# Column blocks in the neighbourhood attention, and VectorE for the rest of each weight unit

## The reference

```python
def _na_mixer(h, hc, w_in, rpb, w_out, need_ctx_out):    # h 512 tokens, hc 256
    q, k, v, g = jnp.split(h @ w_in, 4, axis=-1)          # 16 heads of 64; q * 64**-0.5
    kc, vc = jnp.split(hc @ w_in[:, WIDTH:3 * WIDTH], 2, axis=-1)
    row_idx = ...   # all 8 rows: the window is as high as the grid
    col_idx = clip(col - 8, 0, 64 - 16)[:, None] + arange(16)   # 16 of the 64 columns
    s_loc = (q . k in the window) + rpb[head, row distance, column distance]
    logits = concatenate([s_loc, q . kc], -1)             # 8*16 local keys, 256 context keys
    p = softmax(logits)
    return ((p_loc @ v + p_ctx @ vc) * silu(g)) @ w_out
```

## Time and profile before

| | |
|---|---|
| median of 3 runs | 3138.78 us (3133.11 to 3140.57) |
| the profiled execution, its own time | 3141.7 us |
| its span | 3139.9 us, 37990 instructions |
| mean granted TensorE clock | 0.964 of full speed |
| DMA | 287.38 MB, mean 92 GB/s |

### The profile page before, as it was taken

How to read it: one execution, slowest core, us unless ns; L and a number is a source line. 1 busy time by engine, 2 the same in 40 slices (tenths; PEclk the granted TensorE clock), 3 DMA queues, 4 the chain that set the end, 5 groups by cost and what they waited for, 6 DMA issues and landing times. The chain is left out here.

```text
span 3139.9 us, 37990 instructions
## 1 busy us (share of the span) xinstructions
PE 2919.9 (93%) x14938; PEld 2410.3 (77%) x14938; DVE 1757.9 (56%) x2601; ACT 970.3 (31%) x1552; POOL 803.6 (26%) x304
## 2 busy tenths in 40 slices
PE   7999999999998898888989999999999889999999
PEld 6776777777777776667868888888888668878887
DVE  4984766666645998976556566552233536431111
ACT  2223344444332222223234423122222334332222
POOL 0221212111134443431200022232222120134444
PEclk8998999999999999899989999999999899999999
DMA  5244332232124553432310033331111120022223
GB/s 209 84 148 122 99 93 92 73 99 73 65 101 168 167 168 113 142 114 73 104 58 1 1 101 108 119 104 64 63 61 61 46 81 1 21 74 94 96 98 101
DMA packets 110896, 287.38 MB, mean 92 GB/s; under 512 B 38720, under 2 KB 41888, under 8 KB 110208
## 3 DMA queue, kind: packets, MB, share of 16 engines
q1 hardware_dynamic: 108560, 281.03, 27.0%
q10 hardware_dynamic: 2160, 3.93, 0.4%
HBM read 278.90 MB, written 6.03 MB: 91 GB/s over the span
## 5 line engine op out<-in xcount | busy, mean ns | idle before, releaser
L705 POOL TENSOR_TENSOR w_lo<-w_raw,w_hi 128x1024 fp32r<-128x1024 f32 x300 | 803.4, 2679 | 2325.2 <-ACT w_hi L987 2325.1
L753 PE MATMUL turns<-h_hi,w_hi 128*128 128x512 f32 (+1 forms) x2480 | 811.0, 376 | 86.5 <-POOL w_lo L705 67.9
L753 PE MATMUL turns<-h_hi,w_lo 128*128 128x512 f32 (+1 forms) x2480 | 786.4, 366 | 0.0
L753 PE MATMUL turns<-h_lo,w_hi 128*128 128x512 f32 (+1 forms) x2480 | 784.0, 366 | 0.0
L753 PEld LDWEIGHTS turns<-h_hi,w_hi 128*128 128x128 f32 x2480 | 428.3, 194 | 202.7 <-POOL w_lo L705 89.4
L1204 DVE CUSTOM_DVE_ANT_0 ada_acc<-ada_raw,cond_rows,ada_bias 128x1024 f32<-128x1024 f32 x264 | 501.2, 1923 | 19.3 <-DMA ada_raw<-in_adapack 11.6
L753 PEld LDWEIGHTS turns<-h_hi,w_lo 128*128 128x128 f32 x2480 | 424.0, 193 | 76.3
L753 PEld LDWEIGHTS turns<-h_lo,w_hi 128*128 128x128 f32 x2480 | 425.4, 193 | 73.2 <-issue 1.4
L987 ACT ACTIVATE w_hi<-w_raw 128x1024 fp32r<-128x1024 f32 x300 | 315.4, 1051 | 407.0 <-PE turns L753 389.0
L1195 DVE SCALAR_TENSOR_TENSOR x_lat<-turns,modulation,x_lat 128x512 f32<-128x512 f32 x112 | 83.9, 749 | 413.7 <-PE turns L753 413.7
L753 PE MATMUL turns<-m_hi,w_lo 128*128 128x512 f32 (+1 forms) x768 | 233.4, 358 | 0.0
(11 more groups left out here) (199 smaller groups left out, 3585.1 us busy)
## 6 DMA issues: line engine op xcount, KB each, us to landing
w_raw<-in_wpack SPq DMA_DIRECT2D x300, 512.0 KB, 3.5
ada_raw<-in_adapack SPq DMA_DIRECT2D x176, 512.0 KB, 4.4
bias<-bias_table SPq DMA_DIRECT2D x32, 224.0 KB, 3.8
ada_first_a<-in_adapack SPq DMA_DIRECT2D x12, 512.0 KB, 8.7
bias_table<-bias_out ACTq DMA_DIRECT2D x16, 240.0 KB, 2.4
x_lat<-in_xT SPq DMA_DIRECT2D x1, 2048.0 KB, 8.6
x_ctx<-in_ctxT SPq DMA_DIRECT2D x2, 1024.0 KB, 8.8
ada_first_b<-in_adapack SPq DMA_DIRECT2D x4, 512.0 KB, 14.7
```

Source lines behind the costliest of these rows:

```text
L705: pool.tensor_tensor(Wl[:, b, :], RAW[:, b, :], Wh[:, b, :].bitcast(F32), ALU.subtract).then_inc(w_split, 1)
L753: ins = pe.matmul(dst[:, lo:lo + sz], w, x[:, lo:lo + sz], start=first and n == 0, stop=last and n == 2)
```

## The change

Two things are changed, and a third follows from the space that they need.

**The attention's blocks.** 128 queries are now 8 grid rows of 16 columns, one of four column blocks. Keys and values of the latent tokens are stored in the same order, so that a chunk of 128 keys is a column block too. Block 0 needs chunks 0 and 1, block 1 chunks 0 to 2, block 2 chunks 1 to 3, block 3 chunks 2 and 3, and each the two context chunks 4 and 5:

```diff
+NA_CHUNKS = ((4, 5, 0, 1), (4, 5, 0, 1, 2), (4, 5, 2, 3, 1), (4, 5, 2, 3))
+NA_PLACE = ((0, 1, 4, 5), (0, 1, 2, 4, 5), (4, 5, 1, 2, 3), (4, 5, 2, 3))
+NA_BIAS_AT, NA_BIAS_W = (0, 896, 256, 1280), 1792
# scores, TensorE: 256 or 384 latent columns and 256 of the context
+                            pe.matmul(SP_[:, 0, at_l:at_l + nl], x[:, q], y[:, k0:k0 + nl], start=n == 0, stop=n == 2)
+                            ins = pe.matmul(SP_[:, 0, at_c:at_c + TC], x[:, q], y[:, TX:TT], start=n == 0, stop=n == 2)
# softmax, VectorE and ScalarE: local and context scores lie side by side (nk = 512 or 640)
-                            dve.tensor_tensor_reduce(ex[:, 0:TX], SP_[:, 0, 0:TX], bias, 1.0, -3.0e38, ALU.add, ALU.max,
-                                                     st[:, 0:1])
-                            chain(dve.tensor_reduce(st[:, 1:2], SP_[:, 0, TX:TT], AX.X, ALU.max))
-                            give(dve.tensor_scalar(st[:, 2:3], st[:, 0:1], st[:, 1:2], -1.0, ALU.max, ALU.mult))
+                            give(dve.tensor_tensor_reduce(ex[:, 0:nk], SP_[:, 0, s0:s0 + nk], bias, -1.0, 3.0e38, ALU.add, ALU.min,
+                                                          st[:, 2:3]))
-                            act.activation(ex[:, 0:TX], ex[:, 0:TX], ACT.Exp, bias=st[:, 2:3], scale=1.0, accum_out=st[:, 3:4])
-                            give(act.activation(ex[:, TX:TT], SP_[:, 0, TX:TT], ACT.Exp, bias=st[:, 2:3], scale=1.0,
-                                                accum_out=st[:, 4:5]))
+                            give(act.activation(ex[:, 0:nk], ex[:, 0:nk], ACT.Exp, bias=st[:, 2:3], scale=-1.0,
+                                                accum_out=st[:, 3:4]))
-                            chain(tt(st[:, 5:6], st[:, 3:4], st[:, 4:5], ALU.add))
-                            chain(dve.reciprocal(st[:, 6:7], st[:, 5:6]))
+                        chain(dve.reciprocal(st[:, 6:7], st[:, 3:4]))
# values, TensorE: two blocks at once; a chunk that only one of them needs takes 128 columns
+                        wide = NA_CHUNKS[s.qt + 1 if s.qt == 0 else s.qt]
+                        for n, k in enumerate(wide):
+                            q = slice(0, 256) if n < 4 else slice(P, 256) if s.qt == 0 else slice(0, P)
+                            for j, (v, p) in enumerate(((Vh, PTh[0]), (Vh, PTl[0]), (Vl, PTh[0]))):
+                                ins = pe.matmul(PS[:, b, TT + q.start:TT + q.stop], v[:, k, :], p[:, n, q], ...)
```

The transposes become 4 or 5. Queries, keys, values and gate are put into the new order where they are evicted, and the result goes back into row order:

```diff
+        def by_cols(ap):
+            return ap.rearrange("p (b r c) -> p r b c", b=4, r=ROWS, c=WIN)
+        def by_rows(ap):
+            return ap.rearrange("p (r b c) -> p r b c", b=4, r=ROWS, c=WIN)
# ScalarE, q and k units (the v unit is likewise in two copies, 256 plain and 512 re-ordered)
-                        give(act.activation(dst, ps[:, 0:t], ACT.Copy, scale=0.125 if s.ev == "q" else 1.0))
+                        if s.ev == "k":
+                            act.activation(dst[:, TX:TT], ps[:, TX:TT], ACT.Copy)
+                            give(act.activation(by_cols(dst[:, 0:TX]), by_rows(ps[:, 0:TX]), ACT.Copy))
+                        else:
+                            chain(act.activation(by_cols(T1[:, 0:TX]), by_rows(ps[:, 0:TX]), ACT.Copy, scale=0.125))
+                            give(act.activation(dst[:, 0:TX], T1[:, 0:TX], ACT.Copy))
# ScalarE, g units
-                        give(act.activation(G2[:, s.pair % 2, :], ps[:, 0:t], ACT.Tanh, scale=0.5))
+                        act.activation(by_cols(T1[:, 0:TX]), by_rows(ps[:, 0:TX]), ACT.Copy)
+                        give(act.activation(by_cols(G2[:, s.pair % 2, :]), by_rows(ps[:, 0:t]), ACT.Tanh, scale=0.5))
# VectorE, k and q units
-                        done(rest(lo[:, p, 0:t], ps[:, 0:t], hi[:, p, 0:t], 0.125 if s.ev == "q" else None))
+                        if s.ev == "k":
+                            rest(lo[:, p, TX:TT], ps[:, TX:TT], hi[:, p, TX:TT])
+                            done(rest(by_cols(lo[:, p, 0:TX]), by_rows(ps[:, 0:TX]), by_cols(hi[:, p, 0:TX])))
+                        else:
+                            done(rest(lo[:, p, 0:TX], T1[:, 0:TX], hi[:, p, 0:TX]))
# the result of two blocks
-                        give(act.activation(Oh[r, s.tile, s.q0:s.q0 + 256], PVT[r, :], ACT.Copy))
+                        give(act.activation(blocks(Oh[r, s.tile, :], s.q0), paired(PVT[r, :]), ACT.Copy))
```

The bias of a head is laid out by the host as 128 x 1792 float32 (917 KB, zero for the context columns) and loaded once a head; the `bias_row` steps, their inputs, `bias_table` and the waits on them go:

```diff
-                        for r in range(2):
-                            sp.dma_start(BIAS[n % 2][r * 64:r * 64 + 64, :].rearrange("c (s j) -> c s j", j=GRID_W),
-                                         bias_d[n * NDR + 1 - r:n * NDR + 15 - r].rearrange("s c j -> c s j")
-                                         ).then_inc(bias_in[n % 2], 16)
+                        sp.dma_start(BIAS[n % 2][:], A["bias"][n]).then_inc(bias_in[n % 2], 16)
```

```diff
-        @block.gpsimd
-        def _(pool):
-            for w in range(n_units):
-                b = w % 2
-                pool.wait_ge(w_rounded, w + 1)
-                pool.tensor_tensor(Wl[:, b, :], RAW[:, b, :], Wh[:, b, :].bitcast(F32), ALU.subtract).then_inc(w_split, 1)
+            def split_unit(w):
+                if w < n_units:
+                    dve.wait_ge(w_rounded, w + 1)
+                    if w >= 2:
+                        dve.wait_ge(turn_mm, turn_of_w[w - 2] + 1)
+                    tt(Wl[:, w % 2, :], RAW[:, w % 2, :], Wh[:, w % 2, :].bitcast(F32), ALU.subtract).then_inc(w_split, 1)
...
+                if s.kind == "unit" and turn_of_w[s.w] == s.turn:
+                    split_unit(s.w + 2)
                 if s.ada and s.d1:
                     dve.wait_ge(dve_done, s.d1)
                 for sect, k in s.ada:
```

**Space.** `ada_acc` shrinks from two rows of 1024 to one. The last reduction of a chunk writes its full-width output over its own input (`ada_raw`), and `cond_rows` treats its two rows one after the other:

```diff
+                    dump = ACC[:] if c < both else ADR[:, n % 2, :]
+                    ins = dve.tensor_tensor_reduce(dump, ADR[:, n % 2, :], CROW[:, c, :], 0.5, ADAB[:, sect, k:k + 1],
                                                    ALU.mult, ALU.add, MOD[:, sect, c, k:k + 1])
-                dve.wait_ge(crow_tanh, n)
                 for c in range(2):
-                    ins = stt(CROW[:, c, :], ACC[:, c, :], 1.0, CROW[:, c, :], ALU.add, ALU.mult)
-                ins.then_inc(crow_made, 1)
-                dve.wait_ge(crow_made, n)
+                    dve.wait_ge(crow_tanh, 2 * n - 1 + c)
+                    stt(CROW[:, c, :], ACC[:], 1.0, CROW[:, c, :], ALU.add, ALU.mult).then_inc(crow_made, 1)
+                dve.wait_ge(crow_made, 2 * n)
```

More of the change, by code:

```diff
@@ L205, in na_scores @@
     def na_scores(n, q, k):
-        sc[n] = add("scores", na=True, pair=n // 8, half=n % 8 // 4, qt=n % 4, st=0, eb=n % 2, first=n % 4 == 0, nk=NT)
+        sc[n] = add("scores", na=True, pair=n // 8, half=n % 8 // 4, qt=n % 4, st=0, eb=n % 2, first=n % 4 == 0, nk=len(NA_CHUNKS[n % 4]))
         sc[n].after = [q, k]
     def na_trans(n):
-        tr[n] = add("trans", na=True, eb=n % 2, col=n % 2 * P, nk=NT, qt=n % 4)
+        tr[n] = add("trans", na=True, eb=n % 2, col=n % 2 * P, nk=len(NA_CHUNKS[n % 4]), qt=n % 4)
         tr[n].after = [soft[n - 1]]
@@ L468, in plan @@
     for s in steps:
-        n = {"hnorm": 0, "back": 0, "rope": 1, "vtrans": 1, "scores": s.st, "bias_row": s.st, "trans": 1 if s.na else None}.get(s.kind)
+        n = {"hnorm": 0, "back": 0, "rope": 1, "vtrans": 1, "scores": s.st, "trans": 1 if s.na else None}.get(s.kind)
         if n is not None:
@@ L607, in build_blocks @@
         na_pv_end = [s for s in by_kind["pv"] if s.na][-1]
-        last_gate0 = [s for s in by_kind["unit"] if s.ev == "gate"][KT - 1]
-        first_xupd = [s for s in by_kind["unit"] if s.ev == "xupd"][0]
         first_ctx2 = [s for s in by_kind["sq0"] if s.x0 == TX][0]
@@ L1425, in _ @@
                         take()
-                        done(rest(Ol[r, s.tile, q], PVT[r, :], Oh[r, s.tile, q]))
+                        done(rest(blocks(Ol[r, s.tile, :], s.q0), paired(PVT[r, :]), blocks(Oh[r, s.tile, :], s.q0)))
                     else:
@@ L1453, in _ @@
                         take()
-                        done(stt(G2[:, s.pair % 2, :], G2[:, s.pair % 2, :], 1.0, ps[:, 0:t], ALU.add, ALU.mult))
+                        done(stt(G2[:, s.pair % 2, :], G2[:, s.pair % 2, :], 1.0, T1[:, 0:t], ALU.add, ALU.mult))
                     elif s.ev == "cgate":
@@ L1562, in constants, with bias_places @@
     return c
+def bias_places():
+    at = np.full((ROWS, WIN, NA_BIAS_W), NDR * NDC + 1)
+    for b in range(4):
+        local = sorted(c for c in NA_CHUNKS[b] if c < 4)
+        at0 = NA_BIAS_AT[b] + (0 if b < 2 else TC)
+        for n, chunk in enumerate(local):
+            for r in range(ROWS):
+                for c in range(WIN):
+                    q = b * WIN + c
+                    first = min(max(q - WIN // 2, 0), GRID_W - WIN)
+                    for rk in range(ROWS):
+                        for jc in range(WIN):
+                            j = chunk * WIN + jc
+                            ok = first <= j < first + WIN
```

(2 more changed lines are left out.)

125 lines of the change are left out of this document (48 added, 77 removed).

## The result

The changed kernel takes 3026.3 us (median of 4 runs, 3024.0 to 3035.7), the kernel before 3139.7; ratio 0.9646, 95% interval 0.962 to 0.967. I had forecast 3057 with a range of 3022 to 3098. So the sign and the order are right, and the gain is 113 us where I had worked out 82. The result lies only 4 us inside the lower end of the range and outside the 3040 to 3077 that I gave the likeliest case.

What follows compares the result with a forecast made beforehand. TensorE, busy 93%, was taken to bound most stages, with slack in four stretches and GpSimd's subtraction stalling VectorE. The terms sum to -82 us from 3141.7, giving 3059.9, or 3057 against the median; range 3022 to 3098.

Steps and rivals of the forecast that it cites:

- head, conditioning rows: Conditioning rows, now made one after the other with one scratch: +0.8 us.
- first pool layer, u and gate units: Pool mixer's u units: VectorE now waits for ScalarE's eviction and rounding before subtracting, against the removed stall: +8.7 us.
- bias rows: First pool layer: without its 16 computed bias rows the output projection starts earlier: -16 us (-10 to -18).
- attention: Smaller score, value and transpose work, shorter softmax: -5.6 us in each of seven pairs, last pair -10; -49 (-25 to -75).
- projections and gates that VectorE paces: Output projections of convolution, second pool layer and attention, and second pool gates, lose GpSimd's stall: -15 us (-8 to -25).
- convolution: VectorE loses GpSimd's stalls, TensorE then binds, 182 us against 199: -17 us (-8 to -22).
- second pool layer, u units: VectorE's new wait costs +0.66 us each, 5.3, less 2.1 because first gate units get w_lo sooner: +3.2 us.
- sk and sq, first layer of the second block: Attention and MLP input: rounding, subtraction and reductions end after each other, TensorE waits: +6.5 us (0 to +12).
- all other pairs, norms, second block: First pairs of a stage, where w_lo comes 1 to 1.5 us sooner, with second-block norms: -4 us (0 to -8).
- rival 2: Clock comes back: shorter waits no longer bring it down in the attention and partly the convolution; 3032 us, chance 0.15.
- Rival 1: Attention's gain stays idle: softmax chain sets all steps, -26 there, strided writes up to twice plain rate; about 3085, chance 0.20.
- Rival 3: Subtraction slow on VectorE, 2.44 us instead of 1.22, wherever VectorE paces: +122, 3180 us, chance 0.04.

Runs made afterwards that it cites:

- g: Changed kernel with modulation chunks before the subtraction in units ScalarE evicts alone, and between x update and sum of squares in output projections: 2970.6 us.
- b: Kernel before, with only the w_lo subtraction moved from GpSimd to VectorE; attention, bias table and scratch as before: 3097.5 us, ratio 0.986.
- j: Changed kernel plus five multiplications of constants (256 columns each, never read) on TensorE before the scores of each attention step: 3132.2 us, ratio 0.998.
- k: Changed kernel plus one or two unread multiplications of constants, in turn, on TensorE before the scores of each attention step: 3049.0 us, ratio 0.972.

## Why the forecast came out as it did

Each term of the sum, with what the two profiles show between the same roundings (negative is faster):

| step of the prediction | forecast | measured |
|---|---|---|
| head, conditioning rows | +0.8 | -5.7, by the clock's rise |
| first pool layer, u and gate units | +8.7 | +6.9 |
| bias rows | -16 | -18.6 |
| attention | -49 | -57.9 |
| projections and gates that VectorE paces | -15 | -17.8 |
| convolution | -17 | -18.3 |
| second pool layer, u units | +3.2 | +8.3, their first pair included |
| sk and sq, first layer of the second block | +6.5 | +11.4 |
| all other pairs, norms, second block | -4 | -26.0 |
| sum | -82 | -117.7 |

The head's -5.7 is luck. g has the changed kernel's head, its clock rises at 30.9 us as in the profile of before, and its third rounding starts at 95.03 against 94.35: +0.7, close to the forecast +0.8.

*Right.* The price of the subtraction (1.22 us forecast, 1.22 measured); the reductions at 1.28 (1.24 forecast); MLP units at 8.47 and 5.47; the stages in which the change loses, because VectorE now waits for ScalarE's rounding, and that they are the u, sk and sq units; the bias rows; the convolution. That the gain at the output projections is ordinary pacing is seen in their period: 6.78 became 6.03.

*Losses forecast too small.* Here the clock went the other way. At sk and sq TensorE's idle time grew by 6.7 us, close to the 6.5 of the sum, but the lower level also grew, from 6.8 to 20.5 us, and busy time with it by 4.7: the stage is 11.4 longer. In the second pool layer's u units the idle time grew by 5.2 us (5.3 forecast before I took 2.1 off for the gates) and the lower level by 6.8.

*Attention, 9 us more gain than forecast.* The chain came out about as worked out, the clock did not. A k unit's step, VectorE and TensorE, beside the earlier trace rows:

```profile
513.37 1.02 DVE L1187 TENSOR_TENSOR k_lo<-turns,k_hi 128x256 fp32r<-128x256 f32 x2 [3.23 <-ACT k_hi L1134]
514.31 1.22 DVE L1187 TENSOR_TENSOR w_lo<-w_raw,w_hi 128x1024 fp32r<-128x1024 f32 x1
515.44 1.28 DVE L1201 CUSTOM_DVE_ANT_0 ada_raw<-ada_raw,cond_rows,ada_bias 128x1024 f32<-128x1024 f32 x1
...
516.64 0.82 DVE L1398 CUSTOM_DVE_ANT_0 tmp<-scores,bias 128x640 f32<-128x640 f32 x1
...
518.72 0.56 DVE L1419 TENSOR_SCALAR tmp<-tmp,softmax_stats 128x640 f32<-128x640 f32 x1
...
519.43 0.41 PE L866 MATMUL scores<-k_hi,q_hi 64*128 64x384 f32 x1 [0.97 <-DVE tmp L1419]
```

From the maximum to the next scores it takes 2.8 us (2.85 forecast), and TensorE's wait is 0.97 us, not 1.3. What I left out is what stands behind that: I wrote that enough idle time stays to leave the low-clock part as it is. It did not. In the attention TensorE's clock is at its lower level for 41.0 us before and for 23.9 after. With half the speed missing, that is 8.5 us. Idle time fell by 9.6 (9 forecast), which leaves 39.8 of the 57.9 for the columns (40 forecast). So rival 2 happened by halves, without replacing the likeliest case; a chance for each as if they excluded each other was the wrong form.

*The second block, the largest miss.* I priced GpSimd's stall where modulation chunks are and where TensorE visibly waits for w_lo. The last attention layer has no chunks at all, and it gains 12.3 us. The stretch before and after:

```profile
2461.10:2729.20 268.10, 247.98 (x1381) 201.41 (x1380) 129.32 (x224) 104.60 (x176) 28.35 (x12) 0.96 0.10 32
```

```profile
2358.00:2613.80 255.80, 240.59 (x1380) 195.88 (x1380) 137.18 (x236) 104.69 (x175) 0.00 (x0) 0.99 0.11 34
```

TensorE's idle time falls by 4.9 us and its busy time by 7.4 with the same instructions: again the clock (0.96 to 0.99; its lower level lasts 23.9 us before and 6.8 after, half of the difference is 8.5). The six copies above, 1.39 us each before, stand straight ahead of a multiplication in the head norm that needs their result: TensorE waits for them 8.8 us before and 3.7 after, which is about all of the change in idle time. b shows the same 256.2 us for the stage, so it belongs to the subtraction, not to the attention's blocks. The step of the prediction that failed is the one that costs "the norms of the second block" at -4 in all: it had the copies at nothing, and no term of the sum stood for the clock.

Over the whole kernel after the first unit, the lower level lasts 198 us before and 154 after, half of the difference is 22 us. Of the 36 us between the sum and the two profiles, that is 22 and the head 6; 8 stay open. It is an accounting from the profiles. That filled waits bring the clock up is shown by experiment in j and k, where the lower level in the attention falls from 23.9 us to 0 and 3.4.

*The rivals.* Rival 1 (the gain stays idle, the strided writes slow): no. TensorE's idle time in the attention fell, and j and k show columns on the path. Its arithmetic was off too: 23 and 25 are 48, not 46. The re-ordered copy costs what the plain one does, 128x512 from PSUM before (q_hi) and after (tmp in column blocks):

```profile
L1145 ACT ACTIVATE q_hi<-turns 128x512 fp32r<-128x512 f32 x6 | 3.6, 597 | 9.3 <-PE turns L753 8.2 <-DVE tmp L1416 1.1
```

```profile
L1136 ACT ACTIVATE tmp<-turns 128x512 f32<-128x512 f32 x6 | 3.6, 597 | 12.4 <-PE turns L745 12.4
```

Rival 3 (2.44 us a subtraction): no, 1.22 in all 300. The 7 us that I took for the conditioning rows in the convolution are there (7.12 above), for the loads and the orders behind them.

*The signs.* The 300 subtractions, the reductions (1.29 us at most), the window sums (0.99 at most), the u units and the earlier projection came as written. A pair takes 53.3 us where I had written 55 to 56, and the wait after the k unit shown is 0.97, not 1.3: both miss in the direction of a larger gain.

## What to carry to other kernels

An engine that is 26% busy can cost more than the waits for it show, by what it stops: taking GpSimd out gave 45 us although VectorE got 367 us of work in return. Look for the same operation at two durations (1.28 and 3.37 us here), and count every operation that may be stopped, not only those that one already watches. When work moves into another engine's program, what it costs is set by what it makes that engine wait for, and the cure is order: an independent piece of work ahead of the wait gave back 45 us by the medians. And a forecast in removed waits needs a term for TensorE's clock, which comes back with them.

## What the runs showed of the hardware that I had not expected

- The moment at which TensorE's clock first rises differs from profile to profile, from 19 to 37 us in kernels with the same head, and moves the first unit by up to 10 us. A comparison of two profiles has to start behind it.
- Four subtractions of 128x256 by GpSimd after each rounding, read from one constant tile and waited for by nobody, cost this kernel 106 us. The bias addition of before, which reads PSUM and SBUF, is not slowed by GpSimd's subtraction (0.69 us beside it and away from it).
- Runs of 16 words at a stride cost ScalarE nothing: 597 ns against 597 for 128x512. What the re-ordering does cost is a second instruction: a q unit is now 0.60 and 0.63 us in place of 0.60.
- TensorE at float32 takes 0.45 us for 256 columns in two half passes here (ten in 2.27 us), where an fp32r pass over 256 takes 0.12: a dummy multiplication is not free filler.
